# Where the epsilon of 34 norms is added: from VectorE to GpSimd

## What is computed

```python
def layer_norm(x, g, b):
    mu = jnp.mean(xf, axis=-1, keepdims=True)
    var = jnp.mean(jnp.square(xf - mu), axis=-1, keepdims=True)
    y = (xf - mu) * lax.rsqrt(var + LN_EPS) * g + b
...
x = layer_norm(ALPHA * x + y, ln_g[i, 0], ln_b[i, 0])
```

```python
def rmsnorm(x, g):
    y = xf * lax.rsqrt(jnp.mean(xf * xf, axis=-1, keepdims=True) + NORM_EPS)
...
h = h + merge_heads(heads) @ w_out[layer]
h = h + conv_ffn(rmsnorm(h, norm_ffn[layer]), ...)
return rmsnorm(h, norm_final)
```

## Time and profile before

| what | value |
|---|---|
| median of 3 runs | 2268.27 us |
| lowest, highest run | 2265.27, 2268.65 us |
| the profiled execution's own time | 2265.27 us |
| its span, first to last instruction | 2264.0 us |
| mean granted TensorE clock | 0.975 of full speed |

### The profile page before, as it was taken

How to read it: one execution, slowest core, us unless ns; L and a number is a source line. 1 busy time by engine, 2 the same in 40 slices (tenths; PEclk the granted TensorE clock), 3 DMA queues, 4 the chain that set the end, 5 groups by cost and what they waited for, 6 DMA issues and landing times.

```text
span 2264.0 us, 34071 instructions
## 1 busy us (share of the span) xinstructions
PE 2103.1 (93%) x13749; PEld 1908.1 (84%) x13749; DVE 1543.8 (68%) x2679; ACT 1178.6 (52%) x2027; POOL 70.1 (3%) x126
## 2 busy tenths in 40 slices
PE   7989999898999989999989898998988999999998
PEld 7868899797799978889977778997977999877997
DVE  4665877787677776586777657777465776666776
ACT  4444555493365555455545436554354555465554
POOL 3000000000000010000000000001000000000000
PEclk9999999998999999999999999998898999999999
DMA  8414666455366553456653337654524665534662
GB/s 278 149 56 136 190 184 180 137 164 176 111 196 184 179 155 122 131 173 190 188 161 113 120 105 222 186 181 136 164 75 130 196 186 180 166 96 122 196 187 92
DMA packets 436205, 356.24 MB, mean 157 GB/s; under 512 B 15858, under 2 KB 381686, under 8 KB 436048
## 3 DMA queue, kind: packets, MB, share of 16 engines
q1 hardware_dynamic: 429296, 332.49, 48.5%
q0 software_dynamic: 6752, 21.57, 2.9%
HBM read 352.97 MB, written 1.05 MB: 156 GB/s over the span
## 4 chain that ended last, share of the span: by engine, by line
PE 82%; DVE 10%; ACT 6%; issue 1%; DMA 1%; POOL 0%; SPq 0%; DVEq 0%; ACTq 0%
PE psum L683 20%; PE psum L685 20%; PE psum L684 20%; PE psum L1144 14%; PE psum L1040 3%; DVE w_lo L1706 1%; PE psum L970 1%; ACT e L1535 1%; ACT pt L1547 1%; DVE x_tok L2054 1%; DVE n_tok L2051 1%; DVE xt_lo L1721 1%; PE psum L1026 1%; ACT w_hi L1296 1%; DVE n_tok L2030 1%
## 5 line engine op out<-in xcount | busy, mean ns | idle before, releaser
L1706 DVE TENSOR_TENSOR w_lo<-w_raw,w_hi 128x1024 fp32r<-128x1024 f32 x639 | 751.6, 1223 | 142.1 <-ACT w_hi L1296 140.3
L683 PE MATMUL psum<-xt_hi,w_hi 128*128 128x256 f32 x2744 | 787.3, 287 | 27.9 <-DVE w_lo L1706 19.2
L684 PE MATMUL psum<-xt_lo,w_hi 128*128 128x256 f32 x2744 | 783.5, 286 | 0.0
L685 PE MATMUL psum<-xt_hi,w_lo 128*128 128x256 f32 x2744 | 783.5, 286 | 0.0
L1296 ACT CAST w_hi<-w_raw 128x1024 fp32r<-128x1024 f32 x639 | 646.9, 1049 | 77.9 <-PE psum L685 55.7
L683 PEld LDWEIGHTS psum<-xt_hi,w_hi 128*128 128x128 f32 x2744 | 534.1, 195 | 36.3 <-DVE w_lo L1706 12.4
L684 PEld LDWEIGHTS psum<-xt_lo,w_hi 128*128 128x128 f32 x2744 | 534.0, 195 | 4.7
L685 PEld LDWEIGHTS psum<-xt_hi,w_lo 128*128 128x128 f32 x2744 | 533.6, 194 | 0.0
L2124 DVE SCALAR_TENSOR_TENSOR qt<-psum,par,qt 128x255 f32<-128x255 f32 (+1 forms) x528 | 218.1, 475 | 160.3 <-ACT qt L1604 160.1
L683 PE MATMUL psum<-w_hi,xt_hi 128*128 128x512 f32 (+4 forms) x700 | 263.5, 376 | 13.6 <-DVE xt_lo L1721 12.6
L685 PE MATMUL psum<-w_hi,xt_lo 128*128 128x512 f32 (+4 forms) x700 | 255.1, 364 | 0.0
(11 more groups left out here) (217 smaller groups left out, 1899.3 us busy)
## 6 DMA issues: line engine op xcount, KB each, us to landing
w_raw<-in_f_w_up_dram SPq DMA_DIRECT2D x176, 512.0 KB, 5.0
w_raw<-in_f_w_down_dram SPq DMA_DIRECT2D x88, 512.0 KB, 5.1
w_raw<-in_w_up_dram SPq DMA_DIRECT2D x88, 512.0 KB, 4.8
w_raw<-in_w_down_dram SPq DMA_DIRECT2D x44, 512.0 KB, 5.0
w_raw<-in_x_w_q_dram SPq DMA_DIRECT2D x32, 512.0 KB, 4.2
w_raw<-in_x_w_o_dram SPq DMA_DIRECT2D x32, 512.0 KB, 4.6
w_raw<-in_a_w_qkv_dram SPq DMA_DIRECT2D x24, 512.0 KB, 4.6
w_raw<-in_w_in_fox_dram SPq DMA_DIRECT2D x20, 512.0 KB, 4.6
```

The source lines that it names most:

```text
L683: self.eng.matmul(out, stat[0], mov[0], start=first, stop=False)
L684: self.eng.matmul(out, stat[0], mov[1], start=False, stop=False)
L685: return self.eng.matmul(out, stat[1], mov[0], start=False, stop=last)
L1706: self.up(self.eng.tensor_tensor(self.m.lo[:, s, :], self.m.raw[:, s, :], self.m.hi[:, s, :].bitcast(F32), ALU.subtract), "w_lo", u)
```

## The change

On VectorE the tensor_scalar that adds LN_EPS is gone, and `bn_aggr` itself signals `var`; the instruction that adds the two halves of the squares no longer adds RMS_EPS. On GpSimd one helper, `power`, serves every norm: it waits for the variance, adds the epsilon with a tensor_scalar, waits for its own result, and raises to the power -0.5.

```diff
@@ Vector.norm_part
         if c == 1:
             self.after(n)
-            self.after(self.step(self.eng.bn_aggr(m.norm[:, 2 * b:2 * b + 2], stats[:, b, :])))
-            var = m.norm[:, 2 * b + 1:2 * b + 2]
-            self.up(self.eng.tensor_scalar(var, var, LN_EPS, None, ALU.add), "var", self.tag, b)
+            self.up(self.eng.bn_aggr(m.norm[:, 2 * b:2 * b + 2], stats[:, b, :]), "var", self.tag, b)
@@ Vector.rms_factor
-        self.up(self.eng.scalar_tensor_tensor(part[0], part[0], RMS_EPS, part[1], ALU.add, ALU.add),
-                "var", self.tag, "x", b)
+        self.up(self.eng.tensor_tensor(part[0], part[0], part[1], ALU.add), "var", self.tag, "x", b)
@@ Pool
-    def power(self, r, mean, *which):
-        self.up(self.eng.tensor_tensor(r, mean, self.m.neg_half[:, 0:r.shape[1]], ALU.pow), "rstd", *which)
-
-    def power_of_squares(self, r, mean, *which):
-        self.wait_ge("squared", *which)
-        self.up(self.eng.tensor_scalar(r, mean, RMS_EPS, None, ALU.add), "pool", *which)
-        self.wait_ge("pool", *which)
-        self.power(r, r, *which)
+    def power(self, r, mean, eps, name, *which):
+        self.wait_ge(name, *which)
+        self.up(self.eng.tensor_scalar(r, mean, eps, None, ALU.add), "pool", *which)
+        self.wait_ge("pool", *which)
+        self.up(self.eng.tensor_tensor(r, r, self.m.neg_half[:, 0:r.shape[1]], ALU.pow), "rstd", *which)
...
@@ Pool.norm_part
-            self.wait_ge("var", self.tag, b)
-            self.power(self.m.norm[:, 4 + b:5 + b], self.m.norm[:, 2 * b + 1:2 * b + 2], self.tag, b)
+            self.power(self.m.norm[:, 4 + b:5 + b], self.m.norm[:, 2 * b + 1:2 * b + 2], LN_EPS, "var", self.tag, b)
@@ Pool.stream_power
-        self.wait_ge("var", self.tag, "x", b)
-        self.power(m.norm[:, 20 + b:21 + b], m.norm[:, 16 + 2 * b:17 + 2 * b], self.tag, "x", b)
+        self.power(m.norm[:, 20 + b:21 + b], m.norm[:, 16 + 2 * b:17 + 2 * b], RMS_EPS, "var", self.tag, "x", b)
```

More of the change, by code:

```diff
@@ L2319, in latent_start @@
         self.row(m.third_row[:, C_QR:C_QR + C_KVR], self.t["c_kv_norm"][0], self.tag, "latent")
-        self.power_of_squares(m.norm[:, 14:16], m.norm[:, 12:14], self.tag, "ckv")
-        self.power_of_squares(m.norm[:, 10:12], m.norm[:, 8:10], self.tag, "cq")
+        self.power(m.norm[:, 14:16], m.norm[:, 12:14], RMS_EPS, "squared", self.tag, "ckv")
+        self.power(m.norm[:, 10:12], m.norm[:, 8:10], RMS_EPS, "squared", self.tag, "cq")
     def add_part(self, b, c):
@@ L2346, in second_memory_norm @@
             self.row(m.third_row[:], t["norm_mem_2"][0], self.tag, "mem")
-        self.power_of_squares(m.norm[:, 14:16], m.norm[:, 12:14], self.tag, "mem")
+        self.power(m.norm[:, 14:16], m.norm[:, 12:14], RMS_EPS, "squared", self.tag, "mem")
         self.wait_ge("normed", self.tag, "mem", 1, 1)
```

## The result

| | before | after |
|---|---|---|
| median of 6 runs | 2266.84 us | 2280.61 us |
| lowest, highest | 2265.27, 2268.65 us | 2277.53, 2282.2 us |
| the profiled execution's own time, its span | 2265.27, 2264.0 us | 2280.59, 2279.3 us |
| mean granted TensorE clock | 0.975 | 0.967 |

What follows compares the result with a forecast made beforehand. TensorE's products set the time, except at joints where it waits for a norm. LayerNorms -1.6 (block 1) and -0.7 (block 0), RMS norms +1.5: -0.8 us, from 2268.27 to 2267.5 us; range 2263.5 to 2271.8.

Steps and rivals of the forecast that it cites:

- GpSimd's arm of block 1's LayerNorm: GpSimd's add then power after the aggregation, the later path, letting L2054 start at 169.44 instead of 169.57.
- I take 0.30, the nearest row: Time from GpSimd's one-column add to its power, taken from a two-column add in the latent stage: 0.30 us.
- upper bound of 0.64: Dearest assumed time from GpSimd's add to its power, priced like the power itself: 0.55 + 0.09 us.
- 12 x -0.13: Block 1's 12 LayerNorms on the path: 0.13 of VectorE's 0.19 us stays as gain each, -1.6 us in all.
- Rival 1: GpSimd's add held until VectorE's L2051 ends: +0.59 us per LayerNorm, 2276.2 us in total; chance 0.06.
- Rival 2: TensorE's clock falls at different joints between stages, about 1.45 us per fall, 2266.0 to 2271.8 us; chance 0.18.
- A few of them in either direction: A shift of a tenth of a microsecond may add or remove clock falls: one fewer to three more.
- The price of one fall: Cost of one TensorE clock fall, read from GpSimd's idle times in ffn0 and ffn1: about 1.45 us.
- +7.9: Total change in us if GpSimd's add is held: +7.1 for 12 LayerNorms, -0.7 for `ffn` block 0, +1.5 for RMS norms.
- VectorE's arm: Block 1's LayerNorm on VectorE: L2051 takes L2038's place, 0.19 us earlier, so L2054 could start at 169.38.
- Block 0 in the `ffn` stages: In four stages VectorE's next add starts 0.18 us earlier, overlapping the aggregation: -0.7 us in all.
- The RMS norms: Five of ten on the path, where VectorE waits for the power: +0.30 us each, +1.5 in all; others covered.

Runs made afterwards that it cites:

- the subtraction waits: Changed kernel with L2049 of each LayerNorm waiting for the power, so nothing runs beside GpSimd's add: 2283.75 us, ratio 1.0072.
- the memset: Kernel before with a write-only GpSimd memset of 128 scratch columns ahead of each LayerNorm's power: 2278.12 us in one execution.
- 8-column delay: Kernel before with a VectorE memset of 8 scratch columns in front of block 1's L2055 in each LayerNorm: 2269.66 us, ratio 1.0018.
- 128-column products: Products of zeros, 128 columns wide, filling TensorE's waits for norms: 2263.22 us in the kernel before, 2277.3 us in the changed kernel.

## Why the prediction was wrong

**The step that failed** is GpSimd's arm of block 1's LayerNorm: "I take 0.30, the nearest row". It is 0.86 from add to power (168.58 to 169.44), outside the upper bound of 0.64 too. The number of 0.30 was right for an add that is let through (0.31 in second0, and in the LayerNorms when the subtraction waits); what was wrong is a term that stands nowhere in the sum, the add's wait for L2049's end, taken as nothing: it is 0.56 us (0.78 less 0.22). 12 x -0.13 became 12 x +0.46, 7.1 us of the sum.

**How I came to it.** Rival 1 was the right mechanism, and I gave it 0.06, because in the earlier trace rows the power starts 0.04 behind L2051 and still takes 0.55. I read this overlap as "the engines don't exclude each other". It only shows that a power so close behind can get in; whether one that comes a little later can, it doesn't tell. The trace held the evidence. In the recurrence GpSimd has one product of 1024 columns, and the L1706 beside it took 3.44 us, where the median of all 639 is 1.22:

```profile
470.17 2.75 POOL L2312 TENSOR_TENSOR e<-e,kt 128x1024 f32<-128x1024 f32 x1 [26.66 <-ACT e L1410]
470.57 3.44 DVE L1706 TENSOR_TENSOR w_lo<-w_raw,w_hi 128x1024 fp32r<-128x1024 f32 x1
```

It ended 1.09 after L2312: here VectorE was the one held. At the norm itself the sign is small: L2051 takes 0.77 there, while the second half's, at 170.24 with GpSimd idle, takes 0.74. The durations of this instruction over all its 48 executions (min/median/max in ns), before:

```profile
L2051 DVE SCALAR_TENSOR_TENSOR n_tok<-n_tok,norm,gain_row x48: 733/747/780, 163.2 to 1569.8; 128x512 f32<-128x512 f32 x48
```

and after:

```profile
L2049 DVE SCALAR_TENSOR_TENSOR n_tok<-n_tok,norm,gain_row x48: 734/747/753, 163.1 to 1579.1; 128x512 f32<-128x512 f32 x48
```

Before, the 20 with a power beside them took 0.77 to 0.78, up to 0.03 us more than the others; after, none did, since GpSimd is the one that waits. I passed over both signs. The Trainium skill, SBUF — State Buffer, in the section Who interferes with whom, says that a GpSimd instruction that only writes does not compete with a VectorE instruction with two SBUF inputs, and in the section SBUF: two separate sides, that of two that compete the first keeps the ports to its end. The traces agree with the first: the memset passed in 0.20. With the second they agree where VectorE is first (the power behind that memset was held to 0.97) and for the wide L2312, but not for a power of one column that is first: with the 8-column delay it starts 0.09 ahead of L2055 and runs for 0.55, and L2055 still takes 0.75. What fits is that so small an instruction reads only for a moment, but no row shows that. I had set the page's rule against one row and let the row win; the row spoke only of the case in which GpSimd gets in.

**The size of rival 1.** It had L2054 at +0.59 per LayerNorm, by a full hold of 0.72 plus an add of 0.30 behind it. The held add ends 0.08 after L2049, as if its own work had been done while it waited; measured are 0.46, and 5.5 us instead of 7.1.

**Rival 2** came true as well, and in one direction, which I had said could not be read. "A few of them in either direction" failed: the idle time became longer, and the clock fell in three more joints of the first stack (cross0, cross2, cross3), lower in mix1 to mix3, and within second1 (3.19 us, of which a part may be chance, as said above). As the remainder it makes some 7.5 of the 13.8 us. The price of one fall, 1.45 from the earlier trace rows, was right: from cross0's block 1 to ffn0's the delay grew by 2.20 - 0.51 = 1.69, of which one LayerNorm's 0.46 less block 0's 0.22 is direct, which leaves 1.45 for the fall. What I left out is that rivals 1 and 2 are not alternatives: the delay of the one brings the other. Without that, +7.9 was the most that I saw.

**What held.** VectorE's arm (L2049 0.25 behind the aggregation's start) and the add's start. Block 0 in the `ffn` stages: -0.22 each against -0.18 (L2030 starts 0.18 earlier, as forecast, and takes 0.63 instead of 0.68). The RMS norms: +0.34 each against +0.30, five on the path, the others covered; ffn3's block 1 power came late, after a hold of 2.26, and did no harm there that the rows show. That no transfer is added (each queue has the same packets and bytes). And that taking 24 instructions off VectorE is worth little, since the power was early by only 0.2 us.

**What stays open.** What decides at 50 to 52 ns, and whether the one-input add would get in at 43: it never came so early, and the traces don't show when an instruction reads. Why 128-column products held the clock in before's joints and not in the three of after. And how much of the loss within second1 is due to the change.

## What to carry to other kernels

Before a small instruction is moved to GpSimd, look at what VectorE runs at that moment: if it reads two operands from SBUF, count the small one as held until that one ends, even where today's trace shows an overlap of the two (that one may just have come early enough). And where the granted clock is 1.00 in one joint and 0.7 in its twin, a delay there can have two prices: its own, and that of a fall behind it; test it with a delay alone before arguing about tenths.

## What the runs showed of the hardware that I had not expected

- A GpSimd instruction on 128 elements, held behind two VectorE subtractions in a row, took 2.26 us instead of 0.22; behind L2049 a one-input add ended 0.08 us after the blocker, a held power 0.40 to 0.44.
- Nanoseconds separate a free one from a held one: at 43 to 45 ns behind the subtraction all 74 got in, at 50 and 51 ns 38 of 41, from 52 ns on none. At 0.05 us a power took 0.56 in one place and 1.14 in another of the same profile.
- The hold is uneven. A power of one column that began 0.09 us ahead of the subtraction cost it nothing (0.75); a GpSimd product of 1024 columns made an L1706 take 3.44 us instead of 1.22.
- 0.11 us more before block 1's bias lowered TensorE's clock behind three of four cross stages, and cost 3.1 us where 1.7 were direct.
- 174 products of zeros, 512 columns each, which TensorE had no need of, made the kernel before 10.0 us faster (0.9955 [0.9942, 0.9969]); it is busy for 25.8 us longer on the page (2128.9 against 2103.1), in waits.
